# Stick-breaking scores on both halves of the array's rows, and the convolution's sums of two tiles by accumulating transfers

## What is computed

```python
proj = h @ w_in                       # glu (1024 columns), q k v (3 x 512), gates (2048)
u = u_val * jax.nn.sigmoid(u_gate)    # 512 tokens x 512 channels
u = causal_depthwise_conv(u, conv_w, conv_b)      # 31 taps for each channel
u = jax.nn.silu(layernorm(u, conv_ln_g, conv_ln_b))
y_conv = u @ w_conv_out
# stick-breaking attention, 8 heads of 64:
z = q @ k.T / 8                       # causal: key < query
log_keep = where(causal, log_sigmoid(-z), 0)
log_after = lax.cumsum(log_keep, axis=3, reverse=True) - log_keep
a = where(causal, exp(log_sigmoid(z) + log_after), 0)
o = a @ v
merged = sigmoid(g_conv) * y_conv + sigmoid(g_att) * (o @ w_att_out)
```

## Time and profile before

| | us |
|---|---|
| median of 3 runs | 1374.23 (1372.99 to 1374.35) |
| the profiled execution: its time | 1373.22 |
| its span | 1371.4 |
| PE busy | 1344.5 (98%) |
| DVE busy | 986.8 (72%) |
| ACT busy | 714.9 (52%) |
| POOL busy | 180.9 (13%) |

### The profile page before, as it was taken

The page is one execution under the profiler, slowest core; times in us unless marked ns, Lnnn a source line. Parts: engine busy times, 40 slices in busy tenths (PEclk is TensorE's granted clock), DMA queues, the critical chain, the costliest instruction groups (busy, mean ns, idle before and its releaser), DMA issues.

```text
span 1371.4 us, 19821 instructions
## 1 busy us (share of the span) xinstructions
PE 1344.5 (98%) x7788; PEld 1170.3 (85%) x7788; DVE 986.8 (72%) x1390; ACT 714.9 (52%) x1170; POOL 180.9 (13%) x167
## 2 busy tenths in 40 slices
PE   9999999999999999999999999999999999999997
PEld 7888888788769999998887778887778999998885
DVE  6799899678587878878326764677787788776322
ACT  4466886553475555573224543557465555564221
POOL 3388343200010000004000011121000000000000
PEclk9999999999999999999999999999999999999998
DMA  9422112455701332324532144543221323333221
GB/s 368 146 92 93 47 47 77 148 183 184 299 16 62 100 117 93 122 94 155 176 100 89 62 127 121 133 112 89 95 74 34 121 93 117 100 108 108 92 92 62
DMA packets 45310, 155.98 MB, mean 114 GB/s; under 512 B 6049, under 2 KB 6305, under 8 KB 45090
## 3 DMA queue, kind: packets, MB, share of 16 engines
q1 hardware_dynamic: 42882, 149.70, 32.9%
q0 software_dynamic: 2336, 5.01, 1.6%
HBM read 143.39 MB, written 2.10 MB: 106 GB/s over the span
## 4 chain that ended last, share of the span: by engine, by line
PE 88%; DVE 7%; ACT 3%; issue 1%; POOL 0%; DVEq 0%; ACTq 0%; POOLq 0%
PE ps L1741 27%; PE ps L1742 26%; PE ps L1743 26%; PE ps L1891 1%; DVE t_buf L1098 1%; PE ps L1829 1%; DVE w_lo L1064 1%; PE ps L2157 1%; PE ps L1783 1%; PE ps L1794 1%; PE ps L1795 1%; PE ps L1799 1%; DVE h_lo L1090 1%; ACT w_hi L578 1%; PE ps L2125 0%
## 5 line engine op out<-in xcount | busy, mean ns | idle before, releaser
L1741 PE MATMUL ps<-h_hi,w_hi 128*128 128x256 f32 (+1 forms) x1120 | 374.0, 334 | 3.0 <-ACT sq L806 1.1
L1743 PE MATMUL ps<-h_hi,w_lo 128*128 128x256 f32 (+1 forms) x1120 | 371.6, 332 | 0.0
L1742 PE MATMUL ps<-h_lo,w_hi 128*128 128x256 f32 (+1 forms) x1120 | 371.4, 332 | 0.0
L1064 DVE TENSOR_TENSOR w_lo<-raw,w_hi 128x1024 fp32r<-128x1024 f32 x141 | 183.7, 1306 | 115.6 <-ACT w_hi L578 114.4
L1741 PEld LDWEIGHTS ps<-h_hi,w_hi 128*128 128x128 f32 x1120 | 212.8, 190 | 27.1 <-issue 3.5
L1743 PEld LDWEIGHTS ps<-h_hi,w_lo 128*128 128x128 f32 x1120 | 212.8, 190 | 20.3
L1742 PEld LDWEIGHTS ps<-h_lo,w_hi 128*128 128x128 f32 x1120 | 212.9, 190 | 19.4 <-issue 0.5
L578 ACT ACTIVATE w_hi<-raw 128x1024 fp32r<-128x1024 f32 x141 | 148.1, 1055 | 147.1 <-PE ps L1743 74.0
L1054 DVE TENSOR_TENSOR w_lo<-quads,w_hi 128x1024 fp32r<-128x1024 f32 (+1 forms) x152 | 164.8, 1085 | 72.7 <-ACT w_hi L578 72.7
L578 ACT ACTIVATE w_hi<-quads 128x1024 fp32r<-128x1024 f32 (+1 forms) x152 | 144.3, 949 | 78.2 <-PE ps L1743 76.6
L1741 PE MATMUL ps<-act_hi,w_hi 128*128 128x512 f32 x352 | 137.0, 389 | 0.0
(11 more groups left out here) (316 smaller groups left out, 2262.3 us busy)
## 6 DMA issues: line engine op xcount, KB each, us to landing
quads<-in_ffn_in SPq DMA_DIRECT2D x76, 512.0 KB, 4.5
raw<-in_ffn_out SPq DMA_DIRECT2D x44, 512.0 KB, 3.7
raw<-in_ada SPq DMA_DIRECT2D x32, 512.0 KB, 4.2
raw<-in_qk SPq DMA_DIRECT2D x25, 512.0 KB, 3.7
ada<-in_ada SPq DMA_DIRECT2D x16, 512.0 KB, 7.6
raw<-in_gates SPq DMA_DIRECT2D x16, 512.0 KB, 3.7
raw<-in_v SPq DMA_DIRECT2D x12, 512.0 KB, 3.7
raw<-in_ffn_in SPq DMA_DIRECT2D x12, 512.0 KB, 3.9
```

The lines of the kernel that those rows point to most:

```text
L1064: nc.vector.tensor_tensor(w_lo[SLOT[p]][:], raw[q % RAW][:], w_hi[SLOT[p]][:].bitcast(f32), ALU.subtract).then_inc(raw_used, 1)
L1741: nc.tensor.matmul(out, w[0], v[0], start=start, stop=False, **kw)
L1742: nc.tensor.matmul(out, w[0], v[1], start=False, stop=False, **kw)
L1743: return nc.tensor.matmul(out, w[1], v[0], start=False, stop=stop, **kw)
```

## The change

Scores: `qk_hi` and `qk_lo` become two halves of one tensor `qk_both`. `twin(h)` on POOL's queue copies queries and keys 128 to 511 of head h (both parts) onto the other 64 partitions, two transfers of 192 KB for each head. `scores(n)` takes key block 0 from the head's own rows and blocks 1 to 3 from the copies, with the matmuls of blocks 1 and 0 alternating. It signals `z_done` twice.

Convolution: the 60 adds of POOL become 60 transfers, issued from POOL's queue, that add `tap_buf` (128 partitions of 2 KB) to `conv` in SBUF. The completions are counted on two semaphores `tap_sum`, one for each channel tile, by 16 for a transfer. The waits are otherwise those of before. `TWIN_AT` sets ahead of which sum each head's copies are issued.

```diff
+TWIN_AT = {9: (0, 1), 30: (2,), 33: (3,), 36: (4,), 39: (5,), 42: (6,), 45: (7,)}
...
+            def twin(h):
+                own, other = slice(HD * (h % 2), HD * (h % 2) + HD), slice(HD - HD * (h % 2), P - HD * (h % 2))
+                pool.wait_ge(lo_of["qk1"], 2 * (h // 2) + 2)
+                if h >= 2:
+                    pool.wait_ge(z_done, 2 * (h - 1))
+                nc.gpsimd.dma_start(k_twin[other, :, :].bitcast(f32), qk_both[own, :, 4 + h // 2, P:SEQ].bitcast(f32))\
+                    .then_inc(twin_in[h % 2], 16)
+                nc.gpsimd.dma_start(q_twin[other, :, :].bitcast(f32), qk_both[own, :, h // 2, P:SEQ].bitcast(f32))\
+                    .then_inc(twin_in[h % 2], 16)
+
             for n, (c, j) in enumerate(SUM_ORDER):
+                for h in TWIN_AT.get(n, ()):
+                    twin(h)
                 pool.wait_ge(tap_prod, n + 3)
                 if n >= 2:
-                    pool.wait_ge(pool_tap, n - 1)
-                nc.gpsimd.tensor_tensor(conv[:, c, :], conv[:, c, :], tap_buf[n % 3][:], ALU.add).then_inc(pool_tap, 1)
+                    pool.wait_ge(tap_sum[n % 2], 16 * (n // 2))
+                nc.gpsimd.dma_start(conv[:, c, :], tap_buf[n % 3][:], accum_op=ALU.add).then_inc(tap_sum[n % 2], 16)
...
                     if tapped[0] >= 3:
-                        act.wait_ge(pool_tap, tapped[0] - 2)
+                        act.wait_ge(tap_sum[(tapped[0] - 3) % 2], 16 * ((tapped[0] - 3) // 2 + 1))
...
-                act.wait_ge(z_done, h + 1)
+                act.wait_ge(z_done, 2 * (h + 1))
...
-                for kb in range(NB):
+                other = rows_of(n + 1)
+                pe.wait_ge(twin_in[n % 2], 32 * (n // 2 + 1))
+                hi_lo = (0, 0), (0, 1), (1, 0)
+                for kb, term in ((1, 0), (0, 0), (1, 1), (0, 1), (1, 2), (0, 2),
+                                 (2, 0), (2, 1), (2, 2), (3, 0), (3, 1), (3, 2)):
                     c, at = KEY_BANK[kb]
                     w = SEQ - P * kb
...
+                    a, b = hi_lo[term]
+                    if kb == 0:
+                        key = qk_both[rows, a, 4 + n // 2, 0:P]
+                        query = qk_both[rows, b, n // 2, :]
+                    else:
+                        key = k_twin[other, a, P * (kb - 1):P * kb]
+                        query = q_twin[other, b, P * (kb - 1):SEQ - P]
+                    ins = nc.tensor.matmul(ps[:, 3 * (n % 2) + c, at:at + w], key, query, start=False, stop=term == 2,
+                                           **free)
+                    if term == 2 and kb in (0, 3):
+                        ins.then_inc(z_done, 1)
```

More of the change, by code:

```diff
@@ L175, in build @@
         conv = place("conv", [P, CT, SEQ], f32, at=A0 + 75 * K)
-        qk_hi = place("qk_hi", [P, 8, SEQ], f32r, at=A0)
-        qk_lo = place("qk_lo", [P, 8, SEQ], f32r, at=A0 + 16 * K)
+        qk_both = place("qk_both", [P, 2, 8, SEQ], f32r, at=A0)
+        qk_hi, qk_lo = qk_both[:, 0, :, :], qk_both[:, 1, :, :]
+        q_twin = place("q_twin", [P, 2, SEQ - P], f32r, at=A0 + 63 * K)
+        k_twin = place("k_twin", [P, 2, SEQ - P], f32r, at=t_at + 5 * K)
         v_hi = place("v_hi", [P, NB, SEQ], f32r, at=A0 + 32 * K)
@@ L254, in build @@
         glu_done, glu_sig, u_ready = sem("glu_done"), sem("glu_sig"), sem("u_ready")
-        mod_one, mod_ready, pool_tap = sem("mod_one"), sem("mod_ready"), sem("pool_tap")
+        mod_one, mod_ready = sem("mod_one"), sem("mod_ready")
+        tap_sum = [sem(f"tap_sum{i}") for i in range(2)]
         tap_prod = sem("tap_prod")
@@ L290, in build @@
         both_in, row_in = sem("both_in"), sem("row_in")
-        twin2_in = [sem(f"twin2_in{i}") for i in range(2)]
+        twin_in = [sem(f"twin_in{i}") for i in range(2)]
         s_last = sem("s_last")
@@ L549, in _ @@
                 nc.gpsimd.dma_start(q_twin2[other, :, :].bitcast(f32), m_both[own, :, 8 + i, 0:3 * P].bitcast(f32))\
-                    .then_inc(twin2_in[n % 2], 16)
+                    .then_inc(twin_in[n % 2], 16)
                 nc.gpsimd.dma_start(k_twin2[other, :, :].bitcast(f32), m_both[own, :, 4 + i, 0:3 * P].bitcast(f32))\
-                    .then_inc(twin2_in[n % 2], 16)
+                    .then_inc(twin_in[n % 2], 16)
         @block.scalar
@@ L1942, in _ @@
                     pe.wait_ge(tap, len(TAP_ORDER))
-                    pe.wait_ge(pool_tap, len(SUM_ORDER))
+                    for i in range(2):
+                        pe.wait_ge(tap_sum[i], 16 * (len(SUM_ORDER) // 2))
                     for k in range(CT):
@@ L2111, in softmax_scores @@
                     other = rows_of(n + 1)
-                    pe.wait_ge(twin2_in[n % 2], 32 * ((n - TWIN_FROM) // 2 + 1))
+                    pe.wait_ge(twin_in[n % 2], 32 * (HEADS // 2 + (n - TWIN_FROM) // 2 + 1))
                     for qb, term in ((3, 0), (0, 0), (0, 1), (0, 2), (0, 3), (3, 1), (1, 0), (1, 1), (3, 2), (1, 2),
```

## The result

The changed kernel takes 1398.84 us (median of 4 runs, 1392.08 to 1400.28), beside 1373.64 us for the kernel before on the same chip (1372.99 to 1374.35): a ratio of 1.0174, with a 95% interval of 1.014 to 1.0207. It was forecast at 1367.0, in a range from 1365.5 to 1381.0. The profiled execution took 1398.33 us, of which the span is 1396.5; before, the span was 1371.4. So 25.1 us have to be found.

What follows compares the result with a forecast made beforehand. PE, busy 98% of the span, was taken as the bound. The scores' 5.5 us and the `qk_lo` wait's 1.7 us, with no stall from the sums, took 7.2 off the median 1374.23: 1367.0 us, range 1365.5 to 1381.

Steps and rivals of the forecast that it cites:

- The scores, -5.5 us: Score passes on PE: running both row halves side by side saves 0.69 us in each of eight heads, 5.5 us.
- The rival in which the halves don't pair: Score passes on PE don't overlap, so only 1.7 us goes: 1372.5; chance 0.05 together with DVE not being relieved.
- DVE's relief, -1.7 us: Without POOL's adds DVE's taps run faster, so PE's one wait for `qk_lo` ends: 1.7 us saved.
- L = 3.8 us: Time from a sum's issue until the next of its channel tile may be issued, taken as 3.8 us.
- a stall of 0: PE's loss at the panels of v from slow sums, taken as 0 because 3.8 us is just inside the limit.
- 3.93 allowed: Largest L, in us, at which PE's third panel of v still gets its `w_lo` in time.
- My own formula: PE's stall at v's third panel: each microsecond of L beyond the limit costs 11 us, for eleven chained sums.
- the first rival: Sums too slow, PE waits at the panels of v: 1376.6 at L 4.8, 1381 at 5.2; chance 0.23 above 4.8.
- The sign that was named for it: Forecast wrong first of all if two sums of one channel tile are over 4 us apart.
- The copies "at nothing": PE's wait for the 16 score copies on POOL's queue costs nothing; POOL spends 0.59 us an issue.
- The slower case: Whole kernel ends above 1377.0 us because L exceeds 4.8 us; chance 0.23.
- L = 5.2: Upper bound of L in us, as if reading and writing the target were two transfers in turn; gives 1381.

Runs made afterwards that it cites:

- the fast run: Changed kernel with only sums 33 to 53 as transfers, copies issued from SP's queue, those of heads 6 and 7 earlier: 1367.18 us, ratio 0.9945.

## Why the prediction was wrong, point by point

**The scores, -5.5 us: right.** PE at scores(0) in the changed kernel:

```profile
116.52 0.44 PE L1903 MATMUL ps<-q_twin,k_twin 64*128 64x384 f32 x1
116.52 0.49 PE L1903 MATMUL ps<-qk_both 64*128 64x512 f32 x1
...
117.88 0.50 PE L1757 MATMUL ps<-w_hi,h_hi 128*128 128x512 f32 x1
```

That is 1.36 us in place of the 2.05 of the earlier trace rows, so 0.69 less, as taken; a round of the fast run is 0.70 us shorter. The rival in which the halves don't pair is out.

**DVE's relief, -1.7 us: right in kind.** A tap takes 0.73 to 0.75 us at every one of its 60 calls and no `w_lo` from 60 to 310 us takes over 1.23, beside a DMA share of 0.92. So nothing in the traces shows a transfer slowing DVE. The Trainium skill, "SBUF — State Buffer", section "Who interferes with whom", says that DMA has ports of its own and doesn't contend with the engines; these rows agree. The wait for `qk_lo` shrinks to 1.1 us and does not end, so the term was nearer 0.6.

**L = 3.8 us, and with it a stall of 0: the first step that failed.** L shows in ACT's products. The 24 products of the q and k tiles come to an end here:

```profile
120.31 0.72 ACT L680 ACTIVATE tap_buf<-u_pad,cols 128x512 f32<-128x512 f32 x1 [2.92 <-DMA conv<-tap_buf]
...
126.62 0.72 ACT L680 ACTIVATE tap_buf<-u_pad,cols 128x512 f32<-128x512 f32 x1 [1.79 <-DMA conv<-tap_buf]
127.36 1.28 ACT L580 ACT_TABLE_LOAD   x1
128.66 1.06 ACT L594 ACTIVATE w_hi<-raw 128x1024 fp32r<-128x1024 f32 x1
```

Before, the last product was done at 111.06. Now the last one, product 23, waits for sum 20, the eleventh of its channel tile, until 126.6. The first sum was issued at 73.58 and the copies took 2.4 us (92.19 to 94.61 on POOL), so **L = (126.6 - 73.6 - 2.4) / 11 = 4.6 us**, against 3.8 taken and 3.93 allowed. The `w_hi` that had to start by 121.6 - 1.22 - 1.06 = 119.3 starts at 128.66, 9.4 us late. My own formula gives 11 x (4.6 - 3.93) = 7.4 us, and the chain began 1.75 us later than in the earlier trace rows, together 9.1. The mechanism and its slope were right: it is the first rival. The sign that was named for it, over 4 us between two sums of one channel tile, is there.

The 2.4 us for the copies in this sum are doubtful. With the sums alone, where no copies stand ahead of sum 9, the first sum is issued at 73.61 and product 23 comes no earlier:

```profile
126.35 0.72 ACT L665 ACTIVATE tap_buf<-u_pad,cols 128x512 f32<-128x512 f32 x1 [4.15 <-DMA conv<-tap_buf]
```

That makes L 52.7 / 11 = 4.8 us. So L was 4.6 to 4.8.

Was 3.8 wrong as such? The run with transfers in the rounds and nothing else can tell. There too two of these sums are in flight, but most rounds have hardly a panel's load beside them. Its POOL:

```profile
162.44 1.71 POOL L497 DMA_DIRECT2D conv<-tap_buf  x2 [6.30 <-ACT tap_buf L675]
166.22 0.84 POOL L497 DMA_DIRECT2D conv<-tap_buf  x1 [2.06 <-DMA conv<-tap_buf]
```

The third sum waits for the first of the same channel tile: L = 166.22 - 162.44 = 3.78 us, and 3.79 and 3.80 in the next two rounds. The loads take 1 to 8% of the engines in these stretches. In the first round of the same run, where they take 31%, L is 5.47 us (149.84 to 155.31). So the value from the rows was right for engines that have nothing else to do, and I used it in a stage where they do. The panels hold the engines for 1.3 us of each tile. Added to the 1.5 x 3.78 = 5.67 us of three sums that makes 6.98 us, or L = 4.65 us. This is an estimate which fits the 4.6 to 4.8; no run varies the loads by themselves. The engine time alone would not have shown it: 5.95 us for three sums is an L of 3.97, which by the formula costs 0.4 us. It takes both, the latency with two in flight and the other load on the engines.

The stall also came earlier than the rival had it. PE waits twice while it is still in the q and k tiles, for the `w_lo` of their own panels, whose `w_hi` stands behind products as well:

```profile
100.19 0.47 PE L1757 MATMUL ps<-h_hi,w_hi 128*128 128x512 f32 x1 [1.08 <-DVE w_lo L1080]
109.03 0.66 PE L1757 MATMUL ps<-h_hi,w_hi 128*128 128x512 f32 x1 [3.11 <-DVE w_lo L1080]
```

At v's third panel, where the formula put all of it, only 1.95 us are left (131.03). The three together, 6.1 us and 1.6 at the lower clock, are near the formula's 7.4.

A smaller miss lies beside it: issuing a sum takes POOL 0.85 us and not the 0.59 of a copy.

The Trainium skill, "DMA: Bandwidth & Descriptors", section "Anatomy of one DMA — SWDGE (gpsimd) path", would have given 2.6 us (an estimate, from 2.0 us and the bytes at 436 GB/s); the plain copy measured 3.1 and the adding one 4.3. For a plain copy its figure is near; for an adding one it lies further below than the 3.8 us from the rows did.

**Waits and a clock priced at nothing: the step that put the time outside the range.** By the first rival's formula an L of 4.6 gives 1367.0 + 7.4 = 1374.4, and one of 4.8 gives 1376.6, both inside my range. The measured 1398.84 is 22 to 24 us above. Three places were not in it: the wait for `v_lo` (8.8 us), the wait at the mean (8.2) and the lower clock (7.0).

The v stage. I followed ACT's queue to `w_hi` of v's third panel and stopped. Behind it stand six more products and then `v_hi`. The chain of what ended last goes through three transfers there, one of 7.55 us, before it comes to DVE and PE:

```profile
135.43 7.55 DMA conv<-tap_buf
...
144.85 3.48 DMA conv<-tap_buf
...
148.85 4.38 DMA conv<-tap_buf
...
153.88 0.59 ACT v_hi L636
...
154.49 1.90 DVE v_lo L1205 x3
```

This is the wait of 8.8 us.

The mean. It needs the whole convolution, and the prediction priced no wait there. The chain again:

```profile
257.37 7.88 DMA conv<-tap_buf
...
265.78 5.33 DMA conv<-tap_buf
...
271.64 7.94 DMA conv<-tap_buf
...
279.72 5.40 PE ps L1972 x8
```

Before, PE came to the mean at 254.81 us and did not wait. Now the last three sums of one tile take 22 us, each landing in 5 to 8, beside the loads of the panels behind. This costs PE 8.2 us.

The clock. Every long wait is paid a second time. Behind the one of 8.8 us the 384-wide passes of PE start 0.32 us apart (157.46 and 157.78) and not 0.17 as in the earlier trace rows. In all it is 7.0 us. The rivals priced a wait at its length.

**The copies "at nothing": nearly.** PE never waits for one in the changed kernel. But an issue takes 0.94 us in the median and not 0.59, and with POOL's adds behind it one `w_lo` of 5.56 us went along with it twice, as above.

**The chances.** The slower case got 0.23 and the range ended at L = 5.2, twice a plain copy. That bound held: L was 4.6 to 4.8. The range failed all the same, because its end priced one wait of a chain that has three, and no lower clock. Part of that could be seen before: `v_hi` and the mean stand behind the same products, and the earlier trace rows gave the engines' share in a stage of rounds (0.14), while the sums are densest in that of q and k, where it is 0.24.

The value of the forecast, 1367.0, is what the run with transfers in the rounds alone and copies in time measures (1367.18). The terms of gain were sound in kind, but that the values agree so closely is in part luck: 5.5 us of scores and 0.6 of the wait for `qk_lo` make 6.1 of its 7.0 us.

## What to carry to other kernels

When work moves from an engine to DMA, price it by its latency with as many in flight as there will be, and add what the other transfers of the tightest stage hold the engines for; no landing time on free engines shows that. Follow the queue of each waiting engine to the end of the stretch, not to the first victim, and add the lower clock behind each long wait of PE. Where an operation is too dear in one stage and free in another, split it by stage: 21 of the 60 transfers, those with 12 us for three, together with copies issued in time from SP's queue, kept the gain without the loss.

## What the runs showed that was not expected

- An adding transfer of 256 KB from SBUF to SBUF holds all 16 engines for 1.55 us against 0.68 for a plain copy, in 144 packets against 80, and costs POOL 0.85 us against 0.54 to issue. With half the bytes it is still 144 packets and 0.85 us, and 0.89 us of engine time.
- A DVE instruction that was running as POOL issued two copies and went on with adds took 5.56 us, where 2.31 is usual beside adds. It came once in each of the two runs that had this order (scores alone; transfers in the rounds with POOL's copies) and in none of the four runs with SP's copies and adds in this stage, where the longest is 2.32. Why it comes is not shown.
- The first statistics matmul of PE (`acc,ones_d`) starts at 13.4 to 15.6 us of the profile, though nothing ahead of it was changed: 14.03 before, 15.54 after, 13.87 in the fastest. This moves a comparison by up to 2 us in either direction. As each kernel has one profile, it is not known whether the start belongs to the kernel or to the execution, and its cause was not looked for.
